# A decoder layer with 32 experts: raw rows transposed as they arrive, the norm's factors applied behind the projection, and three smaller moves

## The reference, cut to what matters

```python
h = rmsnorm(x, norm1_g)                      # x * rsqrt(mean(x*x) + 1e-5) * g, per token
q, k, v, u = split(h @ w_in)                 # four products of 1024 x 1024 by 1024 x 512
attn = diff_attention(q, k, v, lam, subln_g) # 4 heads, two causal softmaxes each, subtracted
pool = multiscale_pool(u, w_pool, b_pool, pool_scale)
x = x + concat(attn, pool) @ w_out
h = rmsnorm(x, norm2_g)
logits = h @ router_w + router_b             # 32 experts, top 4 of them per token
x = x + moe(h)                               # clamped SwiGLU, 1024 -> 1024 -> 1024 per expert
y = rmsnorm(x, final_g)
```

## Time and profile before

| | us |
|---|---|
| three runs | 2084.32, 2084.35, 2086.16 |
| median | 2084.35 |
| the profiled execution, its own time | 2084.91 |
| its span, from the first instruction to the last | 2083.2 |
| TensorE busy | 2012.3 (97%) |
| VectorE busy | 651.0 (31%) |

### The profile page before, as it was taken

How to read it: one execution, slowest core, us unless ns; L and a number is a source line. 1 busy time by engine, 2 the same in 40 slices (tenths; PEclk the granted TensorE clock), 3 DMA queues, 4 the chain that set the end, 5 groups by cost and what they waited for, 6 DMA issues and landing times.

```text
span 2083.2 us, 32091 instructions
## 1 busy us (share of the span) xinstructions
PE 2012.3 (97%) x13449; PEld 1644.6 (79%) x13450; DVE 651.0 (31%) x1353; ACT 293.0 (14%) x471; POOL 232.2 (11%) x381
## 2 busy tenths in 40 slices
PE   7999988997899999999999999999999999999996
PEld 4444456554898898889778999988888888989996
DVE  3014667344223222222222322222322222222213
ACT  3001235111011001101100111111110110100103
POOL 0001234122000000100000110010000000010103
PEclk9999999998999999999999999999999999999998
DMA  5210020312978979999999888899989999887855
GB/s 182 81 41 1 0 81 14 148 66 95 343 239 302 321 261 312 325 316 308 327 319 318 310 298 280 279 309 337 317 295 322 320 325 307 282 294 264 288 188 200
DMA packets 231445, 500.83 MB, mean 240 GB/s; under 512 B 7766, under 2 KB 8303, under 8 KB 231298
## 3 DMA queue, kind: packets, MB, share of 16 engines
q1 hardware_dynamic: 218880, 454.46, 60.9%
q0 software_dynamic: 12368, 44.26, 8.6%
q10 hardware_dynamic: 50, 0.01, 0.0%
HBM read 463.63 MB, written 35.13 MB: 239 GB/s over the span
## 4 chain that ended last, share of the span: by engine, by line
PE 73%; DVE 1%; issue 1%; DMA 0%; ACT 0%; POOL 0%; POOLq 0%; DVEq 0%
PE ps L1685 58%; PE ps L1712 12%; PE ps L1699 2%; PE ps L1705 1%; PE ps L1692 1%; DVE x L1253 0%; DMA out<-qk 0%; DMA hT<-h_rows,hT 0%; DVE hT L1246 0%; DVE hT L1240 0%; DVE xn L1220 0%; DVE x L1348 0%; ACT hT L821 0%; PE ps L1865 0%; POOL out L627 0%
## 5 line engine op out<-in xcount | busy, mean ns | idle before, releaser
L1685 PE MATMUL ps<-hT,qk 128*128 128x128 f32 (+8 forms) x4096 | 500.7, 283 | 6.3 <-issue 6.3
L1685 PEld LDWEIGHTS ps<-hT,qk 128*128 128x128 f32 x4096 | 492.5, 192 | 16.1 <-issue 15.4
L1712 PE MATMUL ps<-w_ring,hT 128*128 128x512 f32 x576 | 251.8, 593 | 0.0
L1685 PE MATMUL ps<-hT,u_all 128*128 128x128 f32 (+8 forms) x2048 | 247.7, 282 | 0.0
L1685 PE MATMUL ps<-hT,v 128*128 128x128 f32 (+8 forms) x2048 | 247.7, 282 | 0.0
L1685 PEld LDWEIGHTS ps<-hT,v 128*128 128x128 f32 x2048 | 244.7, 191 | 0.0
L1685 PEld LDWEIGHTS ps<-hT,u_all 128*128 128x128 f32 x2048 | 244.6, 191 | 0.0
L1685 PE MATMUL ps<-hT,w_ring 128*128 128x132 f32 (+7 forms) x1792 | 233.8, 291 | 5.1 <-DVE x L1253 3.8
L1685 PEld LDWEIGHTS ps<-hT,w_ring 128*128 128x128 f32 x1792 | 229.3, 190 | 7.5 <-issue 7.3
L1712 PEld LDWEIGHTS ps<-w_ring,hT 128*128 128x128 f32 x576 | 107.5, 190 | 126.7 <-issue 126.3
L825 ACT ACTIVATE hT<-hT 128x768 f32<-128x768 f32 x64 | 53.8, 841 | 855.0 <-DVE hT L1234 855.0
(11 more groups left out here) (247 smaller groups left out, 1478.5 us busy)
## 6 DMA issues: line engine op xcount, KB each, us to landing
w_ring<-in_w_down SPq DMA_DIRECT2D x64, 2048.0 KB, 7.9
qk<-in_w_gate SPq DMA_DIRECT2D x32, 2048.0 KB, 8.5
qk<-in_w_up SPq DMA_DIRECT2D x32, 2048.0 KB, 10.7
v<-in_w_gate SPq DMA_DIRECT2D x32, 2048.0 KB, 10.6
u_all<-in_w_up SPq DMA_DIRECT2D x32, 2048.0 KB, 8.7
x<-in_b_down SPq DMA_DIRECT2D x32, 512.0 KB, 11.9
w_ring<-in_w_in SPq DMA_DIRECT2D x3, 2048.0 KB, 12.8
x<-in_x SPq DMA_DIRECT2D x8, 512.0 KB, 10.2
```

What stands on the lines that cost most here:

```text
L1685: ins = pe.matmul(bank[:, m, 0:n], w[g][:, k, m * P:(m + 1) * P], rhs[:, k, 0:n], start=k == 0, stop=k == KC - 1)
L1712: ins = pe.matmul(ps[:, 2 * (g % PAIRS), :], aT[:, k, 0:P], w[g][:, k, :], start=k == 0, stop=k == KC - 1)
```

## The change

There are four parts.

1. **Raw rows.** TensorE transposes `x` itself, tile by tile as the DMAs land: seven transposes of each of the tiles 0 to 3 into seven banks, then the eighth job. There is no `xn` at this place and no `norm_rows`. DVE makes the factors behind the evictions (`norm_of`). Two new jobs (`rstd`) spread the factors: TensorE transposes a factor's column, read 128 times over, and ACT copies the bank to `rstd_b`, which has the memory of `g2`. So the load of `g2` moves behind the pooling, ahead of the second half of w_out. All q, k and u banks are now emptied by DVE, with the multiplication by `rstd_b`; v is emptied by ACT with the factor as its scale. The first q products wait for each part of `hT` by itself.
2. **Widths.** DVE makes all ten comparisons in one instruction with a broadcast operand and sums them, ahead of the first expert's tokens. TensorE reads the width and places the hint ahead of the four gate columns of the first expert, no longer behind them.
3. **Exponentials.** In unit 15 ACT does the two exponentials of unit 16 first, then the v bank and the transposed bank.
4. **Tile seven.** DVE norms tile 7 ahead of the last expert's rows.

```diff
-        jobs = rows_n[0] + rows_q[0:4:2] + rows_n[1] + rows_q[4::2] + rows_q[1::2] + rows_k
+        rows_r = [("rstd", q, 0, "act") for q in range(2)]
+        jobs = (rows_n[0] + rows_q[0:1] + rows_r[0:1] + rows_q[2:3] + rows_n[1] + rows_r[1:2] + rows_q[4::2] + rows_q[1::2] + rows_k)
-        rows_u = [("u", h, q, "act" if q else "dve") for h in range(4) for q in range(2)]
+        rows_u = [("u", h, q, "dve") for h in range(4) for q in range(2)]
...
+                        tokens = slice(b * HALF, (b + 1) * HALF)
+                        dve.wait_ge(ev["act"], emptied(number[rows_r[b]])[1])
+                        if what == "q":
+                            ins = dve.scalar_tensor_tensor(qkT[:, 0, a, tokens], bank, DQK ** -0.5, rstd_b[:, tokens], ALU.mult, ALU.mult)
+                        else:
+                            to = qkT[:, 1, a, tokens] if what == "k" else uT[:, a, tokens]
+                            ins = dve.tensor_tensor(to, bank, rstd_b[:, tokens], ALU.mult)
...
+                pe.wait_ge(consts, 5)
+                for t in range(TB // 2):
+                    pe.wait_ge(x_in[t], 16)
+                    for k in range(KC - 1):
+                        ins = pe.transpose(ps[:, bank_of(k), t * P:(t + 1) * P], x[:, t, k * P:(k + 1) * P], ident[:, :])
...
+                    final = u + 1 == UNITS_A
+                    if final:
+                        exps(2 * u + 2)
+                        exps(2 * u + 3)
...
+                o.did(dve.tensor_tensor(over, bcast(tokens, len(WIDTHS) - 1), repeat(steps[:, :], E), ALU.is_gt))
+                o.need()
+                o.did(dve.reduce_sum(width_f, over, axis=AX))
+                o.need()
+                dve.tensor_copy(r.width[:, 1:E + 1], width_f).then_inc(widths_ready, 1)
                 dve.wait_ge(idx_mm, 1)
                 first_tokens(o, tab[0]).then_inc(idx_ready, 1)
...
+                    normed_row(TB - 1)
                     dve.wait_ge(last_in, 32)
...
-                    normed_row(TB - 1)
                     dve.wait_ge(last_sq, nh)
...
                 call(first_hints, first, 0, len(WIDTHS) - 1)
+                pe.wait_ge(gates_done, TB)
+                pe.wait_ge(idx_ready, 1)
+                first_index(slice(2, 6)).then_inc(gate_mm, 1)
```

More of the change, by code:

```diff
@@ L698, in empty @@
                     bank = ps[:, bank_of(n), :]
-                    if what == "norm":
+                    if what == "rstd":
+                        ins = act.activation(rstd_b[:, a * HALF:(a + 1) * HALF], bank, ACT.Copy)
+                    elif what == "norm":
                         if n == 1:
@@ L702, in empty @@
                         ins = act.activation(hT[:, b, a * HALF:(a + 1) * HALF], bank, ACT.Copy, scale=g_in[:, b:b + 1])
[L703 to L706, removed]
-                        ins = act.activation(uT[:, a, b * HALF:(b + 1) * HALF], bank, ACT.Copy)
                     elif what == "v":
@@ L771, in _ @@
                         mix(i - 1)
-                    if u < UNITS_A:
+                    if u < UNITS_A and not final:
                         exps(2 * u + 2)
@@ L906, in norm_rows @@
                     o.need()
-                    dve.sem_inc(normable, end - first)
-                    for b in range(first, first + 2):
-                        dve.tensor_scalar(xn[:, b, :], x[:, b, :], rstd[:, b:b + 1], None, ALU.mult).then_inc(normed["dve"], 1)
-                squares_of(0, TB // 2)
+                    dve.sem_inc(rstd_in, 1)
+                square_of(1)
                 dve.wait_ge(vec_mm, 1)
@@ L947, in _ @@
                     empty(n)
-                squares_of(TB // 2, TB)
-                norm_rows(TB // 2, TB)
+                norm_of(0, TB // 2)
+                dve.wait_ge(consts, 5)
+                o.did(dve.tensor_copy(inv[:, 4, :], inv_i[:, :]))
+                o.need()
+                o.did(dve.reciprocal(inv[:, 4, :], inv[:, 4, :]))
+                o.need()
+                for g in range(POOLS):
+                    o.did(dve.tensor_scalar(inv[:, g, :], inv[:, 4, :], 1.0 / 2 ** (g + 1), None, ALU.max))
+                square_of(5)
+                square_of(7)
+                norm_of(TB // 2, TB)
                 for n in range(KC, 3 * KC):
@@ L1476, in pieces @@
                 def pieces(n):
-                    return {"norm": 4, "pool": 1}.get(jobs[n][0], KC)
-                for n in range(first_late + 1):
+                    return {"norm": 4, "rstd": 4, "pool": 1}.get(jobs[n][0], KC)
+                pe.wait_ge(consts, 5)
[3 more added lines that the diff above has]
+                        ins = pe.transpose(ps[:, bank_of(k), t * P:(t + 1) * P], x[:, t, k * P:(k + 1) * P], ident[:, :])
+                        if t == TB // 2 - 1:
+                            ins.then_inc(job_done, 1)
+                    if t == 1:
+                        pe.wait_ge(vec_in, 80)
+                        pe.transpose(ps[:, 7, 0:25], vec_rows[:, :], ident[0:25, 0:25]).then_inc(vec_mm, 1)
+                pe.wait_ge(vec_ready, 1)
+                for n in range(KC - 1, first_late + 1):
                     product(n, range(pieces(n)))
```

90 lines of the change are left out of this document (33 added, 57 removed).

## The result

The changed kernel takes 2073.22 us (median of 5 runs, 2071.99 to 2074.92) against 2084.35 (5 runs, 2084.27 to 2086.97): a ratio of 0.9945, with a 95% interval from 0.9934 to 0.9956. I had forecast 2070.0. The profiled execution is the slowest of the five, 2074.92 with a span of 2073.2; stages are compared with it, and differences of under 1 us in one stage are taken with care.

The account below looks back on a forecast made before the run. The prediction took TensorE, busy 2012.3 of 2083.2 us, to bound the kernel, with gains only from its idle time and lower clock. Terms 6.8 + 3.0 + 4.1 + 0.4 = 14.3 us gave 2070.0 us, range 2065.5 to 2077.

Parts of the forecast that it names:

- Part 1: At the start, transposes follow the landing tiles and the third q product comes earlier: 6.8 us, between 5.4 and 8.9.
- the clock's term: At the start, q's first product was expected to run partly at 1.2 GHz, taking back 2.1 of 8.9 us.
- Evictions: DVE empties all q, k and u banks; at 0.7 to 0.8 us each, 1.6 at worst, hidden, so no cost.
- an "issue" ahead of a later expert: Sign against the forecast: idle time named "issue" standing ahead of an expert after the first.
- Part 3: In the attention, the 2.3 us wait for ACT goes and the clock may stay up: 3.0 us, between 2.0 and 3.9.
- it doesn't add up: Rival: gaps close but the time returns because a later stage waits for DMA; 2077.5 us, chance 0.06.
- Part 2: Ahead of the first expert, earlier widths and hint remove the 5.57 us gap: 4.1 us, between -0.4 and 5.2.
- if the earlier hint covers it: Step at the first expert's jump: an earlier hint covers the code load, so the expert starts about 520.4, 4.7 us earlier.
- The first rival: The gap at the first expert's jump stays, leaving a gain of 10.2 us, 2073.9 us; chance 0.24.
- Part 4: At the end, tile 7 is sent earlier but lands hardly earlier, DMA being full: 0.4 us, between 0 and 1.8.
- the start is held: Rival: a bank DVE empties too late holds the transposes of tiles 4 to 7; 2072.3 us, chance 0.08.
- other jumps: Rival: bodies move in the code, each later jump no longer covered costs 5.57 us; four give 2092; chance 0.04.

Follow-up runs that it names:

- start_only: The changed kernel with the widths, exponentials and tile seven parts undone, so that only the raw rows part stands: 2075.96 us, ratio 0.9956.
- banks: The changed kernel with the two banks of the late jobs in the other order (3, 1 instead of 1, 3): 2072.08 us, ratio 0.9934.
- touch: The changed kernel without the first hint, with TensorE jumping once into the first expert's body and straight back when the width is read: 2074.82 us, ratio 0.996.
- pad: The changed kernel with never-executed instructions, 48 ahead of the walk to the first hint and 202 behind the first jump: 2069.55 us, ratio 0.9928.
- no_hint: The changed kernel without the walk that ends at the first hint, the jump itself as before: 2081.20 us (12 runs), ratio 0.9979.
- moved: The changed kernel with never-executed instructions, 1 and 168, nearly all behind the first jump, so only the experts' bodies move: 2087.66 us (11 runs), ratio 1.0012.
- late_hint: The changed kernel with the walk to the first hint moved between the two halves of the first expert's transposes: 2069.29 us, ratio 0.9922.

## Why the prediction was near, and where it was wrong

The sign, the order of size and three of four mechanisms were right. The sum was 3.2 us too large, and that near only because the errors in parts 1 and 2 have opposite signs: luck, not accuracy.

*Part 1 (6.8 forecast; 9.0 measured alone, 9.31 less 0.9 in the trace).* The mechanism is as described: transposes from 4.62, and w_in's load sets the first product (12.23, forecast 12.7). Mis-sized is the clock's term of 2.1 us. The first 14 transposes take 0.23 us each, the next seven 0.14, and q's first product 7.13 against 7.03 for the second. So by the durations the level rose by 8.2, and the product paid 0.1 us and not 2. (The granted clock in the windows is 1.00 from the start in both kernels, so only the durations show this rise.) I had carried over the 6 to 7 us from the kernel before, whose rise I had placed by its products' start. The rest is the load of w_in, which landed 0.5 us before my 12.7 here and 1.4 before it in `start_only`.

*Evictions ("Nothing").* Wrong by 0.88 us, shown by `banks`. I had asked whether DVE is fast enough, and not which bank each job gets when two jobs are put in ahead. I had named a wait for DVE in the attention as a sign against the forecast, and it is there, small. The other such sign, an "issue" ahead of a later expert, is there only with 0.26 and 0.50 us ahead of a first product (949.35 and 1510.96); the kernel before has 0.30 and 0.46 of this kind (1474.90 and 1521.22), which I had read as no gap.

*Part 3 (3.0; 2.5 measured).* Right: the wait of 2.3 is gone and comes back with the edit undone, and the level stays up. In the traces the stage gives more, 3.7 us up to the routing, of which part is lost ahead of the experts. This is the rival "it doesn't add up" in small.

*Part 2 (4.1; 0.2 by the medians, whose sign the runs don't settle).* Here the prediction failed, at the step "if the earlier hint covers it". That the gap is the load of the jump's target was right (`touch`). That an earlier hint helps was wrong: the hint acts by where it lies in the program, and moving it back in time also moved it back in the code. The first rival, that the gap stays, is what happened; it gave 2073.9 (its own gain of 10.2 us makes 2074.2 from 2084.35). Part 2's upper end of 5.2 had no row behind it: the gap could give 525.13 - 520.19 = 4.9 at most. The rule behind the rival, that a taken branch pays and prefetch is sequential only, is the Trainium skill's (Runtime: NRT & Kernel Launch, Instruction fetch mechanics). It gives the right time here, and `pad` contradicts it as a rule: there a hint covers a jump of this size.

*Part 4 (0.4; nothing measured).* Right, for the reason given: 7.57 us to land instead of 5.67.

*The rival "the start is held".* It did not happen: the rows from 12.23 to 30.44 follow each other without a wait.

*The rival "other jumps".* In the changed kernel no later jump was uncovered to a degree that costs: it is 10.04 us ahead at the first expert's index product and 10.13 at the 31st. I gave it 0.04 since the distance between hint and jump inside a body is unchanged. But that is not what counts: `no_hint` and `moved` leave these distances alone too and lose 8 and 14 us. That the change left them covered was luck, and 0.04 was too little.

Open: the exact bound at which a hint stops acting. That the place in the program decides is shown; that it is a block's bound between hint and jump is a guess, which fits `pad`, `late_hint` and the changed kernel with either order of part 2, but the one run that should have placed losses by it (`moved`) put them elsewhere. Also open is why the stretch from routing to the first expert varies between 27.9 and 30.4 us in kernels that are nearly alike there.

## What to carry to other kernels

When TensorE idles under the name "issue" at a jump or in the middle of a product whose operands are there, suspect the load of code. Look in the DMA view for a packet of an "instruction" queue inside the idle time, and try instructions that are never executed ahead of the place before reordering work. After any edit that changes the number of instructions, compare the start of each later stage with the version before: a difference that appears only there belongs to the code's place and not to the edit. When a job is put into a list that deals out banks by number, look up which jobs now share a bank.

## What the runs showed of the hardware

A hint executed some 9 us ahead of its jump had no effect in one place of the program (gap 6.09 us, no instruction packet before it) and a full one 50 instructions further on (two packets at 498 to 500, no gap beyond the 0.98 for ACT). Moving bodies of code without changing them moved the time from 2073 to 2088 us (`moved`). A stall of 2 to 3 us inside a product goes with a granted clock below 1 (0.72 in 1740 to 1745 of `no_hint`); the stalls of 0.4 to 1.1 us in `moved` left it at 1.00 (950 to 955, 1280 to 1285). And a gain ahead of a stretch with waits on DMA and a low clock need not reach its end: of 3.74 us 1.20 were left 30 us later in one pair of traces, and 2.77 of 3.76 in another.
